# Two passes over the input channels in a layer's first projection, with its modulation rows read by column halves

## The chip, the cores and the metric

The program runs on one core of one Trainium2 chip. The metric is the device time of one execution in microseconds, the median of several runs. Besides its span (first to last instruction) an execution has a little more time around it. The engines are named as in the profile: PE is TensorE, with PEld for its weight loads, DVE is VectorE, ACT is ScalarE, POOL is GpSimd, SP is SyncE, which here only issues DMAs.

## What is computed

Two transformer layers over 256 tokens of width 2048, batch 1, in 32-bit floats. The change touches the start of the first:

```python
def hybrid_layer(x, c, rel_table, w_ada, b_ada, pre_g, post_g, w_in, sink,
                 w_pool_grp, pool_scale, w_br_attn, w_br_pool, w_merge, b_merge, w_out):
    mod = jax.nn.silu(c) @ w_ada + b_ada
    shift, scale, gate = jnp.split(mod, 3, axis=-1)
    h = rmsnorm(x, pre_g) * (1.0 + scale[:, None]) + shift[:, None]
    proj = h @ w_in
    q, k, v, gate_a, u, gate_p = jnp.split(proj, SPLIT_POINTS, axis=-1)
    ...
    g = jax.nn.sigmoid(h @ w_merge + b_merge)
    ...
    o = merged @ w_out
    return x + gate[:, None] * rmsnorm(o, post_g)
```

`w_ada` is 2048 x 6144 (its thirds give shift, scale and gate), `w_in` is 2048 x 4608. Nothing of `h @ w_in` can start before shift and scale are known for the input channels that it uses. The second layer has six such modulation vectors, from `w_mod`.

## The kernel before

**Weights.** Every large weight is read once, in slabs of 1 MB: 512 input channels (4 chunks of 128) by 512 columns. A slab lands in one of five slots of `w_stage` (SP, L557). ACT rounds it into `w_hi` (L779, two halves of 128x1024, three buffers), DVE takes the remainder, `w_lo = w_stage - w_hi` (`split_lo`, L1110, two halves). PE multiplies both, the three products of a split operand. SP issues slab n+3 while PE is at slab n, ACT and DVE split slab n+2 (`AHEAD`). `w_hi` of slab n+2 has to wait until PE has used slab n-1.

**Column groups.** `w_in` has nine groups of 512 columns, each four slabs deep, in the phases in 0, u0, u1, in 1 to 3, in_gates 0 and 1, gate_p1. A group fills all four banks of the tile `gemm` in PSUM, in two pairs. When a pair is complete ACT copies its low half into `proj` (L779), DVE adds the high half (L1501), and only then may PE start the next group in that pair (`wait_banks`). The first pair is complete in the middle of the group's last slab.

**Modulation.** A product with one row `c` is done on DVE: for each of the 16 chunks of channels one row of 128 x 2048 (1 MB) is read and accumulated with its `silu(c)` (`mod_acc`, L1088). 16 rows give a part, that is, one vector. PE then sums over partitions (16 products of 128x128 by 128x1, L1597 and L1842). Parts 0 and 1 (shift, scale) are done in the opening, 32 rows, through four of the slots of `w_stage`. Then come the 16 tiles of the operand: DVE scales (L1198), ACT makes the high part, DVE the low part (L1202). All later parts are hidden behind the matmuls: `mod_row` (L1104) reads a row in two halves of 512 KB through the two buffers of `mod_stage` (SP, L580), each reloaded once DVE has consumed it. `mod=(part, first row, rows)` and `slots` of a phase say at which slabs.

**What sets the order.** Each engine runs the same list of phases in order. At each slab DVE does `split_lo` of the slab two ahead, the phase's hooks (pooling, attention), its modulation row if any, and, at a group's last slab, the evacuation. SP issues the slab three ahead and then the modulation row. Phases after the nine: merge 0 to 7 (four slabs each, with one attention head hidden in each), branch1 0 to 3, out1 0 to 3, then the second layer.

## Time and profile before

| | us |
|---|---|
| median of 3 runs (2324.1 to 2327.34) | 2326.93 |
| the profiled execution | 2325.86 |
| its span | 2324.1 |
| PE busy / DVE busy / ACT busy in the span | 2217.0 / 1692.8 / 1062.4 |
| first matmul of `gemm` starts at | 106.94 |
| first matmul of the merge phases starts at | 330.71 |

PE is the busiest engine. A busy PE is not always a fast one: the rows of stretches carry the granted clock, 1.00 for its higher level (2.4 GHz) and 0.50 for its lower (1.2 GHz). Rows of a timeline say when a piece starts, how long it takes, and in brackets for how long the engine had been idle and what ended that.

### The profile page before, as it was taken

The numbers are of one execution on the slowest core, as the hardware profiler recorded it, in microseconds if no ns is written. First come the engines' busy times: TensorE is split into PE (matmuls) and PEld (weight loads), VectorE is DVE, ScalarE is ACT, GpSimd is POOL, SyncE is SP. The second block draws the span as 40 slices with busy tenths as digits, with TensorE's granted clock in tenths as the row PEclk, the third lists the DMA queues.
The fourth block names the chain that finished last, engine by engine and source line by source line (L and its number), as shares of the span: only waits on it lengthen the run. The fifth ranks groups of instructions, "written<-read, shape, count | busy, mean of one in ns | idle before, by whom it ended". The sixth has DMA issues, their size and how long they took to land.

```text
span 2324.1 us, 27765 instructions
## 1 busy us (share of the span) xinstructions
PE 2217.0 (95%) x11184; PEld 1863.6 (80%) x11184; DVE 1692.8 (73%) x1981; ACT 1062.4 (46%) x1345; POOL 74.7 (3%) x109
## 2 busy tenths in 40 slices
PE   5499999999999999999999999999999999999998
PEld 2388888888878878788878878878888888888886
DVE  6858867787777777767786887568888886774444
ACT  4143345554346654453455633455444443443432
POOL 0000000100000000000011100000000000000000
PEclk8599999999999999999999999999999999999999
DMA  9878778888985756669877888656676665657553
GB/s 381 332 249 299 277 259 312 297 313 309 313 289 198 252 173 227 233 204 329 288 268 242 286 319 277 237 201 216 218 242 229 235 219 175 204 182 253 188 193 127
DMA packets 244932, 583.49 MB, mean 251 GB/s; under 512 B 11994, under 2 KB 14830, under 8 KB 239428
## 3 DMA queue, kind: packets, MB, share of 16 engines
q1 hardware_dynamic: 232560, 535.93, 66.5%
q0 software_dynamic: 11104, 43.37, 5.5%
q10 hardware_dynamic: 1140, 2.43, 0.3%
q8 instruction: 88, 1.44, 0.2%
q14 instruction: 40, 0.33, 0.0%
HBM read 562.78 MB, written 18.90 MB: 250 GB/s over the span
## 4 chain that ended last, share of the span: by engine, by line
PE 79%; DVE 10%; DMA 7%; ACT 2%; issue 1%; ACTq 0%; DVEq 0%
PE gemm L1816 22%; PE gemm L1777 13%; PE gemm L1779 13%; PE gemm L1778 13%; PE gemm L1817 11%; DVE w_lo L1110 3%; DMA mod_stage<-in_w_mod 3%; DMA w_stage<-in_w_ada 2%; DVE mod_acc L1104 2%; DMA mod_stage<-in_w_ada 1%; PE gemm L1820 1%; PE extra L1597 1%; DVE mod_acc_scale L1088 1%; PE gemm L1819 1%; ACT w_hi L779 1%
## 5 line engine op out<-in xcount | busy, mean ns | idle before, releaser
L1110 DVE TENSOR_TENSOR w_lo<-w_stage,w_hi 128x1024 fp32r<-128x1024 f32 x730 | 861.5, 1223 | 432.5 <-ACT w_hi L779 432.1
L779 ACT ACTIVATE w_hi<-w_stage 128x1024 fp32r<-128x1024 f32 x730 | 731.4, 1051 | 831.1 <-PE gemm L1779 403.8
L1816 PE MATMUL gemm<-operand_main,w_hi 128*128 128x512 f32 x2535 | 912.3, 402 | 15.8 <-DVE proj L1501 14.4
L1817 PE MATMUL gemm<-operand_main,w_lo 128*128 128x256 f32 x2535 | 715.1, 282 | 0.0
L1816 PEld LDWEIGHTS gemm<-operand_main,w_hi 128*128 128x128 f32 x2535 | 480.7, 190 | 129.9 <-DVE w_lo L1110 15.3
L1817 PEld LDWEIGHTS gemm<-operand_main,w_lo 128*128 128x128 f32 x2535 | 483.1, 191 | 7.5
L1777 PE MATMUL gemm<-w_hi,operand_main 128*128 128x512 f32 x960 | 381.6, 398 | 7.3 <-DVE operand_main L1262 5.8
L1778 PE MATMUL gemm<-w_lo,operand_main 128*128 128x512 f32 x960 | 376.4, 392 | 0.0
L1779 PE MATMUL gemm<-w_hi,operand_main 128*128 128x512 f32 x960 | 376.1, 392 | 0.0
L1104 DVE SCALAR_TENSOR_TENSOR mod_acc<-mod_stage,c_silu,mod_acc 128x1024 f32<-128x1024 f32 x180 | 229.0, 1299 | 58.6 <-DMA mod_stage<-in_w_mod 43.0
L1777 PEld LDWEIGHTS gemm<-w_hi,operand_main 128*128 128x128 f32 x960 | 181.8, 189 | 46.9 <-issue 9.8
L1779 PEld LDWEIGHTS gemm<-w_hi,operand_main 128*128 128x128 f32 x960 | 181.8, 189 | 38.2
L1778 PEld LDWEIGHTS gemm<-w_lo,operand_main 128*128 128x128 f32 x960 | 181.9, 189 | 37.0
L1777 PE MATMUL gemm<-w_hi,ffn_hidden 128*128 128x512 f32 x352 | 136.9, 389 | 0.0
L1778 PE MATMUL gemm<-w_lo,ffn_hidden 128*128 128x512 f32 x352 | 136.9, 389 | 0.0
L1779 PE MATMUL gemm<-w_hi,ffn_hidden 128*128 128x512 f32 x352 | 136.9, 389 | 0.0
L1777 PE MATMUL gemm<-w_hi,operand_attn 128*128 128x512 f32 x256 | 101.6, 397 | 2.1 <-DVE w_lo L1110 2.1
L1778 PE MATMUL gemm<-w_lo,operand_attn 128*128 128x512 f32 x256 | 101.0, 395 | 0.0
L1779 PE MATMUL gemm<-w_hi,operand_attn 128*128 128x512 f32 x256 | 100.9, 394 | 0.0
L1779 PEld LDWEIGHTS gemm<-w_hi,ffn_hidden 128*128 128x128 f32 x352 | 66.1, 188 | 13.8
L1778 PEld LDWEIGHTS gemm<-w_lo,ffn_hidden 128*128 128x128 f32 x352 | 66.1, 188 | 13.8
L1777 PEld LDWEIGHTS gemm<-w_hi,ffn_hidden 128*128 128x128 f32 x352 | 66.1, 188 | 13.5
(231 smaller groups left out, 1744.5 us busy)
## 6 DMA issues: line engine op xcount, KB each, us to landing
w_stage<-in_w_in SPq DMA_DIRECT2D x129, 1024.0 KB, 6.2
mod_stage<-in_w_mod SPq DMA_DIRECT2D x192, 512.0 KB, 6.1
w_stage<-in_w_up SPq DMA_DIRECT2D x88, 1024.0 KB, 5.0
w_stage<-in_w_down SPq DMA_DIRECT2D x44, 1024.0 KB, 5.0
w_stage<-in_w_merge SPq DMA_DIRECT2D x32, 1024.0 KB, 6.1
w_stage<-in_w_out SPq DMA_DIRECT2D x32, 1024.0 KB, 7.8
w_stage<-in_w_ada SPq DMA_DIRECT2D x31, 1024.0 KB, 7.6
mod_stage<-in_w_ada SPq DMA_DIRECT2D x32, 512.0 KB, 6.0
```

The costliest lines, as they stand in the source:

```text
L779: return nc.scalar.activation(o, i_, f, **kw)
L1088: ins = stt(acc[:, c0:c1], row, CSI[:, t % 16:t % 16 + 1], acc[:, c0:c1], ALU.mult, ALU.add)
L1104: stt(acc, MST[:, half, :], CSI[:, c:c + 1], acc, ALU.mult, ALU.add).then_inc(mod_rows, 1)
L1110: tt(WL[:, slot_of(n), c0:c1], WST[:, slot_of(n), c0:c1], WH[:, n % HIS, c0:c1].bitcast(F32), ALU.subtract)\
L1597: ins = mm(X[3][:, t:t + 1], acc[:, t * P:(t + 1) * P], ONES[:, 0:1], start=True, stop=True)
L1777: mm(o, x_hi, hi, start=(k == 0), stop=False)
L1778: mm(o, x_hi, lo, start=False, stop=False)
L1779: ins = mm(o, x_lo, hi, start=False, stop=(k == nk - 1))
L1816: mm(G[:, m, :], hi, x_of(k), start=(k == 0), stop=False)
L1817: ins = mm(G[:, m, T:2 * T], lo, x_of(k)[:, 0:T], start=False, stop=False)
L1819: mm(G[:, m, T:2 * T], lo, x_of(k)[:, 0:T], start=False, stop=False)
L1820: ins = mm(G[:, m, :], hi, x_of(k), start=False, stop=True)
```

## The change

The rows of `w_ada` that are needed first are read by column halves. In the opening 16 rows are read instead of 32: each has the first 1024 columns of shift and the first 1024 of scale. That gives shift and scale for input channels 0 to 1023, operand tiles 0 to 7. The nine groups of `w_in` then run twice. Pass one (phases "half" 0 to 8) takes slabs 0 and 1 of each group and leaves the partial sum in `proj` (`part`). Under its first sixteen slabs the second halves of the 16 rows are read, two pieces of 512 KB each, through four buffers (`ada_stage`), and accumulated by DVE (`second_half`). In phase half 8 PE sums them over partitions (`ada_end`), and tiles 8 to 15 follow (`tiles`). Pass two takes slabs 2 and 3 of each group; its evacuation is done by DVE alone, two additions per pair (`rest`). The gate rows (part 2), which stood at 16 slabs of these nine groups, have 5 places left in pass two; the other 11 move into merge 0 to 3, and the rows of parts 3 and 4 move back behind them: merge 0 to 7 take 24 rows (16 before), branch1 0 to 3 take 12 (8 before), out1 7 (8 before). The column sums of part 2 move from the end of gate_p1 to the end of merge 3, those of part 3 from merge 7 to branch1 0. In the opening the eight products for the position bias (`line_rows`) are made in three portions with two buffers, and four products of the identity with `line_rows` are put before the column sums, into a bank that nobody reads. On POOL's queue the loads for the pooling now wait for operand tile 15, and the store of the bias lines stands behind them.

```diff
+        half = lambda c: Group(w_in, c, 2, "main", "part", tile=c // P)
+        rest = lambda c: Group(w_in, c, 2, "main", "rest", chunk0=KT // 2, tile=c // P)
...
-        pool = lambda n: {0: [("pool_sum", n)], 1: [("pool_mix", n)], 2: [("pool_out", n)]}
-        phases.append(Phase("in", 0, [one(0)]))
-        phases.append(Phase("u0", 0, [one(2560)]))
-        phases.append(Phase("u1", 0, [one(3072)]))
+        first_cols = (0, 2560, 3072, 512, 1024, 1536, 2048, 3584, 4096)
+        for n, c in enumerate(first_cols):
+            phases.append(Phase("half", n, [half(c)], ada=2 * n if n < 8 else None,
+                                hooks={0: [("ada_end", 0)], 1: [("ada_end", 1), ("tiles", 2)]} if n == 8 else {}))
+        phases.append(Phase("in", 0, [rest(0)], mod=(2, 0, 1), slots=(0,), hooks={0: [("tiles", 3)]}))
+        phases.append(Phase("u0", 0, [rest(2560)], mod=(2, 1, 1), slots=(0,)))
+        phases.append(Phase("u1", 0, [rest(3072)], mod=(2, 2, 1), slots=(0,)))
         for n, c in enumerate((512, 1024, 1536)):
-            phases.append(Phase("in", n + 1, [one(c)], mod=(2, 3 * n, 3), slots=(0, 2, 1), hooks=pool(n)))
-        for i in range(2):
-            phases.append(Phase("in_gates", i, [one(2048 + 1536 * i)], mod=((2, 9, 3), (2, 12, 3))[i],
-                                hooks={} if i else pool(3), post=[]))
-        phases.append(Phase("gate_p1", 0, [one(4096)], mod=(2, 15, 1), slots=(1,), post=[("mod_end", 2), ("silu1", 0), ("v1", 0)]))
+            phases.append(Phase("in", n + 1, [rest(c)], hooks={0: ([("pool_out", n - 1)] if n else []) + [("pool_sum", n)], 1: [("pool_mix", n)]}))
+        phases.append(Phase("in_gates", 0, [rest(2048)], hooks={0: [("pool_out", 2), ("pool_sum", 3)], 1: [("pool_mix", 3)]}))
+        phases.append(Phase("in_gates", 1, [rest(3584)], hooks={0: [("pool_out", 3)]}, mod=(2, 3, 1), slots=(0,)))
+        phases.append(Phase("gate_p1", 0, [rest(4096)], mod=(2, 4, 1), slots=(0,), post=[("silu1", 0), ("v1", 0)]))
...
-                                mod=(3, 2 * i, 2), slots=(0, 2),
-                                post=[("mod_end", 3)] if i == 7 else []))
+                                mod=(2, 5 + 3 * i, 3) if i < 3 else ((2, 14, 2), (3, 0, 3), (3, 3, 3), (3, 6, 3), (3, 9, 4))[i - 3],
+                                slots=(0, 1, 2, 3) if i != 4 else (1, 2, 3), post=[("mod_end", 2)] if i == 3 else []))
...
-                                hooks=behind, mod=(4, 2 * i, 2), slots=(0, 2)))
+                                hooks=behind, mod=(4, 3 * i - 3, 3) if i else (3, 13, 3), slots=(0, 1, 2),
+                                post=[] if i else [("mod_end", 3)]))
...
-                                hooks=behind, mod=(4, 8 + 3 * i, (3, 3, 2, 0)[i]), post=[("resid", 0)] if i == 3 else []))
+                                hooks=behind, mod=(4, (9, 12, 14, 16)[i], (3, 2, 2, 0)[i]), post=[("resid", 0)] if i == 3 else []))
...
-        MOD0_ROWS = 32
+        MOD0_ROWS = 16
...
+        AST = [MST[:, 0, :], MST[:, 1, :], proj_tile("ada_stage2", [P, D // 2], F32, 36)[:, :], proj_tile("ada_stage3", [P, D // 2], F32, 44)[:, :]]
...
+                src = w.rearrange("(c q) (p n) -> c q p n", q=P, n=D)[t, :, 0:2, 0:D // 2]
+                dst = WST[:, t % ROW_SLOTS, :].rearrange("q (p n) -> q p n", p=2)
...
+            def load_second_half(r):
+
+                if r == 0:
+                    sp.wait_ge(x_sq, 2)
+                for part in range(2):
+                    j = 2 * r + part
+                    positive(sp, ada_rows, j - 3)
+                    sp.dma_start(AST[j % 4], A["w_ada"][0].rearrange("(c q) n -> c q n", q=P)[r, :, part * D + D // 2:(part + 1) * D])\
+                        .then_inc(ada_landed[j % 4], 16)
...
+                if part == 2 and row0 + r == 0:
+                    sp.wait_ge(ada_rows, 32)
...
             for n in range(1, LEAD):
                 load_slab(n)
+                load_second_half(n - 1)
             for ph in phases:
                 for s in range(len(ph.slabs)):
                     if ph.slab0 + s + LEAD < len(slabs):
                         load_slab(ph.slab0 + s + LEAD)
+                    if ph.ada is not None and ph.ada + s + 2 < KT:
+                        load_second_half(ph.ada + s + 2)
                     for r in mods_behind(ph, s):
                         load_mod_row(ph, r)
...
-            pool.wait_ge(slab_used, 2)
-            pool.wait_ge(line_copied, HEADS1)
-            pool.dma_start(lines[:, 0:P * LINE].rearrange("h (q k) -> q h k", q=P), LINEB[:, :, :]).then_inc(start["lines_stored"], 16)
             pool.wait_ge(vec_copied, NP)
-            pool.wait_ge(start["lines_stored"], 16)
+            pool.wait_ge(ada_rows, 32)
+            pool.wait_ge(op_ready, op_count["prep_h0b"])
             pool.dma_start(WP[:, :, :, :], A["w_pool_group"][0].rearrange("g (c q) d -> q g c d", q=P))\
                 .then_inc(start["pool_in"], 16)
             pool.dma_start(INVC[:, :, :].rearrange("q g n -> q (g n)"), A["k_invcnt"][0].partition_broadcast(P))\
                 .then_inc(start["pool_in"], 16)
+            pool.wait_ge(line_copied, HEADS1)
+            pool.dma_start(lines[:, 0:P * LINE].rearrange("h (q k) -> q h k", q=P), LINEB[:, :, :]).then_inc(start["lines_stored"], 16)
 
...
+                    make_lines(7, HEADS1)
+                    act.wait_ge(half_modv, 2)
+                    high_tiles(0)
+                    split_hi(1)
+                    high_tiles(1)
+                    split_hi(2)
                     split_hi(3)
...
+            def second_half(r):
+
+                for part in range(2):
+                    j = 2 * r + part
+                    dve.wait_ge(ada_landed[j % 4], 16 * (j // 4 + 1))
+                    positive(dve, ada_rows, j - 1)
+                    acc = MACC1[:, part * (D // 2):(part + 1) * (D // 2)]
+                    if r == 0:
+                        ins = ts(acc, AST[j % 4], CSI[:, 0:1], None, ALU.mult)
+                    else:
+                        ins = stt(acc, AST[j % 4], CSI[:, r:r + 1], acc, ALU.mult, ALU.add)
+                    ins.then_inc(ada_rows, 1)
...
-            first_rows(0, 25)
+            first_rows(0, 13)
             norm_rs(0)
-            stage_mod_end(0)
-            first_rows(25, 28)
+            first_rows(13, 15)
             split_lo(0)
-            first_rows(28, MOD0_ROWS)
+            first_rows(15, MOD0_ROWS)
...
                 if what == "prep_h" and k == 0:
-                    base = 0
-                    src, src0, shift = PROJ, XT0, 0
                     scale_half(0)
...
+                    scale_tile(0)
+                    half_sums(0, 0)
+                    scale_tile(1)
+                    for t in range(2, 10):
+                        if t < 8:
+                            scale_tile(t)
+                        low_tile(t - 2)
+                        if t == 7:
+                            split_lo(1)
+                    split_lo(2)
+                    split_lo(3)
...
+                if name == "ada_end" and arg == 1:
+                    scale_half(1)
+                    half_sums(1, 0)
+                if name == "tiles":
+                    if arg == 2:
+                        scale_tile(8)
+                        scale_tile(9)
+                    for t in range(4 * arg, 4 * arg + 4):
+                        if t + 2 < KT:
+                            scale_tile(t + 2)
+                        low_tile(t)
...
-                    dve.wait_ge(lo_out, g.low0 + u + 1)
-                    if g.evac == "proj":
+                    if g.evac != "rest":
+                        dve.wait_ge(lo_out, g.low0 + u + 1)
+                    if g.evac in ("proj", "part"):
                         o = PROJ[:, g.kw["tile"] + 2 * u:g.kw["tile"] + 2 * u + nt, :]
+                        tt(o, high, o, ALU.add).then_inc(pair_done, 1)
+                    if g.evac == "rest":
+                        o = PROJ[:, g.kw["tile"] + 2 * u:g.kw["tile"] + 2 * u + 2, :]
+                        wait_evac(dve, part_of[g.col], u + 1)
+                        wait_full(dve, g, u)
+                        link(tt(o, half_of(g, u, 1), o, ALU.add))
                         tt(o, high, o, ALU.add).then_inc(pair_done, 1)
...
+                    if ph.ada is not None:
+                        second_half(ph.ada + s)
...
+                if name == "ada_end" and arg == 0:
+                    pe.wait_ge(ada_rows, 32)
+                    pe.wait_ge(half_modv, 2)
+                    ada_sums(MACC1, 1, 1, mod_summed)
+                    ada_sums(MACC1, 1, 0, mod_summed)
...
-            mod_end(0)
-            for half in range(2):
-                pe.wait_ge((half_row, mod0_rows)[half], (1, MOD0_ROWS)[half])
-                if half:
-                    pe.wait_ge(line_copied, HEADS1)
-                for t in range(8 * half, 8 * half + 8):
-                    ins = mm(X[2 - half][:, t:t + 1], MACC1[:, t * P:(t + 1) * P], ONES[:, 0:1], start=True, stop=True)
-                ins.then_inc((half_summed, mod_summed)[half], 1)
+            pe.wait_ge(mod0_rows, LAST_ROW - 1)
+            pe.wait_ge(line_copied, HEADS1)
+            for n in range(4):
+                mm(X[0][:, :], IDENT[:, :], LINEB[:, n, :], start=True, stop=True)
+            pe.wait_ge(half_row, 1)
+            ada_sums(MACC, 0, 1, half_summed)
+            pe.wait_ge(mod0_rows, MOD0_ROWS)
+            ada_sums(MACC, 0, 0, half_summed)
```

The opening on DVE, before: 32 rows (the first two entries of each part's 16, then `w_lo` of slab 0 between rows), then the sums' results `mod_cols` and the operand tiles.

```order
L1086 TENSOR_SCALAR mod_acc<-w_stage,c_silu 128x2048
L1088 SCALAR_TENSOR_TENSOR mod_acc<-w_stage,c_silu,mod_acc 128x2048 x15
L1086 TENSOR_SCALAR mod_acc_scale<-w_stage,c_silu 128x2048
L1088 SCALAR_TENSOR_TENSOR mod_acc_scale<-w_stage,c_silu,mod_acc_scale 128x2048 x8
L1115 RECIPROCAL rstd<-rstd 128x256
L1070 TENSOR_TENSOR mod_cols<-extra,columns 128x16
L1088 SCALAR_TENSOR_TENSOR mod_acc_scale<-w_stage,c_silu,mod_acc_scale 128x2048 x3
L1110 TENSOR_TENSOR w_lo<-w_stage,w_hi 128x1024 x2
L1088 SCALAR_TENSOR_TENSOR mod_acc_scale<-w_stage,c_silu,mod_acc_scale 128x2048 x3
L1088 SCALAR_TENSOR_TENSOR mod_acc_scale<-w_stage,c_silu,mod_acc_scale 128x1024 x2
L1136 TENSOR_TENSOR mod_cols<-extra,columns 128x8
```

And after:

```order
L1124 TENSOR_SCALAR mod_acc<-w_stage,c_silu 128x2048
L1126 SCALAR_TENSOR_TENSOR mod_acc<-w_stage,c_silu,mod_acc 128x2048 x12
L1166 RECIPROCAL rstd<-rstd 128x256
L1126 SCALAR_TENSOR_TENSOR mod_acc<-w_stage,c_silu,mod_acc 128x2048 x2
L1161 TENSOR_TENSOR w_lo<-w_stage,w_hi 128x1024 x2
L1126 SCALAR_TENSOR_TENSOR mod_acc<-w_stage,c_silu,mod_acc 128x1024 x2
L1185 TENSOR_TENSOR mod_cols<-extra,columns 128x8
L1194 SCALAR_TENSOR_TENSOR affine_cols<-mod_cols,columns 128x8
L1202 SCALAR_TENSOR_TENSOR quad_work<-proj,affine_cols,rstd 128x256
L1185 TENSOR_TENSOR mod_cols<-extra,columns 128x8
L1202 SCALAR_TENSOR_TENSOR quad_work<-proj,affine_cols,rstd 128x256 x2
L1207 SCALAR_TENSOR_TENSOR operand_main<-quad_work,mod_cols,operand_main 128x256
```

Half of the row instructions are gone from ahead of `mod_cols`; the reciprocal, `w_lo` and the tiles stand as close to the end of the rows as before.

The steady part of the nine groups on DVE, before (two groups without modulation rows: u0 and u1):

```order
L1110 TENSOR_TENSOR w_lo<-w_stage,w_hi 128x1024 x4
L1501 TENSOR_TENSOR proj<-gemm,proj 128x512 x2
L1110 TENSOR_TENSOR w_lo<-w_stage,w_hi 128x1024 x8
L1501 TENSOR_TENSOR proj<-gemm,proj 128x512 x2
L1110 TENSOR_TENSOR w_lo<-w_stage,w_hi 128x1024 x8
L1501 TENSOR_TENSOR proj<-gemm,proj 128x512 x2
```

After, in pass one (one group of two slabs and the start of the next):

```order
L1161 TENSOR_TENSOR w_lo<-w_stage,w_hi 128x1024 x2
L1139 SCALAR_TENSOR_TENSOR mod_acc_second_half<-mod_stage,c_silu,mod_acc_second_half 128x1024 x2
L1161 TENSOR_TENSOR w_lo<-w_stage,w_hi 128x1024 x2
L1139 SCALAR_TENSOR_TENSOR mod_acc_second_half<-ada_stage_97,c_silu,mod_acc_second_half 128x1024
L1139 SCALAR_TENSOR_TENSOR mod_acc_second_half<-ada_stage_98,c_silu,mod_acc_second_half 128x1024
L1575 TENSOR_TENSOR proj<-gemm,proj 128x512 x2
L1161 TENSOR_TENSOR w_lo<-w_stage,w_hi 128x1024 x2
```

Between the last `w_lo` of a group and the additions that free its banks (`proj<-gemm,proj`) now stand two row pieces, and a group ends after two slabs, not four.

The start of the merge phases' second head on DVE, before:

```order
L1104 SCALAR_TENSOR_TENSOR mod_acc<-mod_stage,c_silu,mod_acc 128x1024 x2
L1110 TENSOR_TENSOR w_lo<-w_stage,w_hi 128x1024 x2
L1387 TENSOR_TENSOR y_work<-extra,proj 128x256
L1392 TENSOR_TENSOR operand_attn<-y_work,operand_attn 128x256
L1358 SCALAR_TENSOR_TENSOR scores<-extra,bias 128x512
L1362 TENSOR_REDUCE small<-scores 128x2
L1367 TENSOR_SCALAR small<-small,sinks 128x2
L1110 TENSOR_TENSOR w_lo<-w_stage,w_hi 128x1024 x2
L1373 TENSOR_TENSOR small<-small 128x2
L1375 RECIPROCAL small<-small 128x2
L1380 TENSOR_SCALAR scores<-scores,small 128x256 x2
L1104 SCALAR_TENSOR_TENSOR mod_acc<-mod_stage,c_silu,mod_acc 128x1024 x2
```

After:

```order
L1155 SCALAR_TENSOR_TENSOR mod_acc<-mod_stage,c_silu,mod_acc 128x1024 x2
L1161 TENSOR_TENSOR w_lo<-w_stage,w_hi 128x1024 x2
L1460 TENSOR_TENSOR y_work<-extra,proj 128x256
L1465 TENSOR_TENSOR operand_attn<-y_work,operand_attn 128x256
L1431 SCALAR_TENSOR_TENSOR scores<-extra,bias 128x512
L1435 TENSOR_REDUCE small<-scores 128x2
L1440 TENSOR_SCALAR small<-small,sinks 128x2
L1155 SCALAR_TENSOR_TENSOR mod_acc<-mod_stage,c_silu,mod_acc 128x1024 x2
L1161 TENSOR_TENSOR w_lo<-w_stage,w_hi 128x1024 x2
L1446 TENSOR_TENSOR small<-small 128x2
L1448 RECIPROCAL small<-small 128x2
L1453 TENSOR_SCALAR scores<-scores,small 128x256 x2
```

Each merge phase has one more row of two pieces, behind the attention step at its second slab.

## Rows read from the trace of the kernel before

**Rows 1.** page: busy by engine; the group of line 779: busy us, mean ns
```profile
PE 2217.0 (95%) x11184; PEld 1863.6 (80%) x11184; DVE 1692.8 (73%) x1981; ACT 1062.4 (46%) x1345; POOL 74.7 (3%) x109
...
L779 ACT ACTIVATE w_hi<-w_stage 128x1024 fp32r<-128x1024 f32 x730 | 731.4, 1051 | 831.1 <-PE gemm L1779 403.8
```

**Rows 2.** TensorE in order of time, opening: start us, us, line, operation
```profile
100.10 6.99 PE L1842 MATMUL extra<-ones,mod_acc_scale 128*128 128x1 f32 x32 [32.50 <-DVE mod_acc_scale L1088]
...
106.94 0.77 PE L1816 MATMUL gemm<-operand_main,w_hi 128*128 128x512 f32 x1
```

**Rows 3.** VectorE in order of time, opening
```profile
45.41 12.27 DVE L1088 SCALAR_TENSOR_TENSOR mod_acc<-w_stage,c_silu,mod_acc 128x2048 f32<-128x2048 f32 x5 [0.15 <-DMA w_stage<-in_w_ada]
...
80.08 1.75 DVE L1115 RECIPROCAL rstd<-rstd 128x256 f32<-128x256 f32 x1
...
89.13 2.35 DVE L1110 TENSOR_TENSOR w_lo<-w_stage,w_hi 128x1024 fp32r<-128x1024 f32 x2
...
103.71 0.17 DVE L1136 TENSOR_TENSOR mod_cols<-extra,columns 128x8 f32<-128x8 f32 x1 [2.47 <-PE extra L1842]
...
105.30 0.48 DVE L1202 SCALAR_TENSOR_TENSOR operand_main<-quad_work,mod_cols,operand_main 128x256 fp32r<-128x256 f32 x1
```

**Rows 4.** VectorE in order of time, ends of two quiet column groups
```profile
150.44 2.36 DVE L1110 TENSOR_TENSOR w_lo<-w_stage,w_hi 128x1024 fp32r<-128x1024 f32 x2 [3.30 <-ACT w_hi L779]
...
152.75 0.69 DVE L1501 TENSOR_TENSOR proj<-gemm,proj 128x512 f32<-128x512 f32 x1
...
175.36 0.69 DVE L1501 TENSOR_TENSOR proj<-gemm,proj 128x512 f32<-128x512 f32 x1
```

**Rows 5.** VectorE in order of time, end of a group with modulation rows
```profile
250.19 1.28 DVE L1104 SCALAR_TENSOR_TENSOR mod_acc<-mod_stage,c_silu,mod_acc 128x1024 f32<-128x1024 f32 x1 [2.34 <-DMA mod_stage<-in_w_ada]
...
251.39 2.35 DVE L1110 TENSOR_TENSOR w_lo<-w_stage,w_hi 128x1024 fp32r<-128x1024 f32 x2
...
253.66 1.28 DVE L1501 TENSOR_TENSOR proj<-gemm,proj 128x512 f32<-128x512 f32 x2
```

**Rows 6.** TensorE in order of time: two waits for banks, and sums of columns
```profile
202.66 0.47 PE L1816 MATMUL gemm<-operand_main,w_hi 128*128 128x512 f32 x1 [0.96 <-DVE proj L1501]
...
254.49 0.47 PE L1816 MATMUL gemm<-operand_main,w_hi 128*128 128x512 f32 x1 [2.90 <-DVE proj L1501]
...
326.83 3.63 PE L1597 MATMUL extra<-ones,mod_acc 128*128 128x1 f32 x32
```

**Rows 7.** stretches: us, busy of PE, PEld, DVE, ACT, POOL, clock, DMA share, GB/s
```profile
110.00:115.00 5.00, 5.00 (x23) 4.30 (x22) 5.00 (x10) 2.99 (x7) 0.00 (x0) 0.74 0.00 0
...
202.00:203.00 1.00, 0.34 (x2) 0.33 (x3) 1.00 (x2) 1.00 (x2) 0.00 (x0) 1.00 1.06 424
...
256.00:257.00 1.00, 1.00 (x4) 0.86 (x4) 1.00 (x2) 0.00 (x0) 0.00 (x0) 0.50 1.04 391
...
331.00:335.00 4.00, 4.00 (x12) 3.15 (x11) 4.00 (x2) 4.00 (x4) 0.00 (x0) 0.57 0.16 61
```

**Rows 8.** DMA issues: out<-in, queue, count, KB each, median us to landing
```profile
w_stage<-in_w_in SPq DMA_DIRECT2D x129, 1024.0 KB, 6.2
...
mod_stage<-in_w_mod SPq DMA_DIRECT2D x192, 512.0 KB, 6.1
...
w_stage<-in_w_ada SPq DMA_DIRECT2D x31, 1024.0 KB, 7.6
```

**Rows 9.** who waited for whom, 200 to 310: us in total, times, longest
```profile
PE gemm L1816 <- DVE proj L1501: 5.3, 5, 2.9
```

**Rows 10.** stretches of a merge phase, and of the second and last branch phase
```profile
379.00:403.00 24.00, 24.00 (x110) 19.92 (x108) 18.62 (x23) 13.73 (x18) 2.13 (x4) 1.00 0.89 308
...
571.00:583.00 12.00, 12.00 (x54) 9.95 (x53) 10.82 (x12) 4.02 (x4) 0.53 (x1) 1.00 0.95 351
...
619.00:631.00 12.00, 12.00 (x58) 9.98 (x57) 11.93 (x13) 4.99 (x6) 1.24 (x2) 1.00 1.05 398
```

**Rows 11.** TensorE in order of time, out1 phase
```profile
645.19 0.76 PE L1777 MATMUL gemm<-w_hi,operand_main 128*128 128x512 f32 x1 [3.87 <-DVE operand_main L1262]
```

154 lines of the change are left out of this document (81 added, 73 removed).

## The prediction, made before the changed kernel was run

> **What bounds the kernel now.** I read the page first: PE is busy for 95% of the span [rows 1], so time is to be had where PE is empty or slow. The largest such place is the opening. PE's first matmul of the projection starts at 106.94; ahead of it PE summed columns for 6.99 us and before that sat idle for 32.50 us, waiting for DVE's `mod_acc_scale` [rows 2]. DVE at that time works without a break on 1 MB rows, five of them in 12.27 us, 2.45 us each [rows 3]. So the start is set by 32 rows, and each row less is worth 2.45 us. Next I read the ends of column groups: quiet ones repeat every 22.61 us (152.75 to 175.36) [rows 4], which is 5.65 us per slab; where modulation rows stand on DVE, PE waited for its banks, 5.3 us in five waits, the longest 2.9 us [rows 9]. Last I read the clock: the 0.96 us wait at 202.66 left the granted clock at 1.00, the 2.90 us wait at 254.49 was followed by 0.50 [rows 6, 7].
>
> **Opening.** The twelfth row starts at 45.41, so thirteen are done at 50.3 [rows 3]. The new order goes on with the reciprocal (1.75), two rows (4.9), `w_lo` (2.35): 59.3. The last row comes in two halves of 1.28 each [rows 5]; the scale half is done at 60.6, the shift half at 61.9. Eight column sums take half of 6.99 us at the low clock [rows 2] or half of 3.63 us at the high one [rows 6]. I take the high one: four 128x512 products now run just before, and in the kernel before the projection's own matmuls brought the clock from 0.50 back up within the stretch from 110 to 115 [rows 7]. The sums end at 60.6 + 1.8 + 1.8 = 64.2. From `mod_cols` to the end of the first low tile it was 105.30 + 0.48 - 103.71 = 2.1 us [rows 3], with two scalings now moved behind; I take 1.7. The first matmul starts at 65.9, **41.0 us earlier**; at the low clock it would be 69.4, 37.5 earlier. The bias lines leave this path: they are done before the rows, as now.
>
> **Start of pass one.** Now DVE has to bring seven more tiles (an estimate of 0.8 us each for two instructions of 0.48 that overlap [rows 3]), `w_lo` of slabs 1 to 3 (3 x 2.3), and four row pieces (two plain ones at 0.7, two at 1.25, estimates from rows 5) before it frees the first bank: 65.9 + 5.6 + 6.9 + 3.9 = 82.3. PE restarts 0.83 us after the addition begins (253.66 to 254.49 [rows 5, 6]): 83.1. Its own work of two slabs would end at 65.9 + 11.3 = 77.2. That is 5.9 lost, plus a clock drop, as after the 2.90 us wait. I price a drop by the stretch from 331 to 335 at 0.57, 43% of 4 us, 1.7 [rows 7]. Against it, before, the projection itself began at 0.50: clock 0.74 over 110 to 115 [rows 7] puts the rise at 112.6, so 2.8 us of loss are gone. Together **+4.8**.
>
> **The seven further group ends of pass one.** A slab's end lets ACT round the next high part (1.05 us a half [rows 1]), so `w_lo` starts about 1.2 us after it and takes 2.31 us to the next instruction [rows 4]: 3.5. Before, the addition followed at once. Now two row pieces, 2.5 us, stand between: the addition begins 6.0 and PE restarts 6.8 us after the slab's end, where the slab needs 5.65. Each group loses 1.15 us, **+8.1** in all. Such a gap is like that of 202.66, so no clock drop. The low bound is 0 (waits vanish); the high bound comes from loads. Each slab's issue on SP now stands behind a row piece that waits for a buffer. DVE consumes the group's last piece 5.65 + 6.0 = 11.7 us after the group's start; then the slab for the next critical place is issued, and it is needed when the next group has used its first slab, at 12.45 + 5.65 = 18.1, 6.4 us later. Landing takes a median 6.2, in the opening's full queue 7.6 [rows 8]; at 7.6 it is 1.2 us more per group, 16.5 in all.
>
> **Column sums in phase half 8.** 16 products, 3.63 us [rows 6], now inside the stream, and with a clock drop like the one that followed them at 331 [rows 7], 1.7 us: **+5.3**. Nothing hides them, PE is the engine that they occupy. DVE uses the time: tiles 8 to 11 end before the slab does.
>
> **Pass two.** DVE needs two additions of 0.69 [rows 4] per pair, begins 3.5 us after a slab's end and is done at 5.0, within 5.65. So 0.6 us cover is left, and the 5.3 us of bank waits [rows 9] with one clock drop (1.7) go, as no rows stand at the end of those groups. I leave 0.6 for the pooling groups: **-6.4**. ACT loses its copies there. POOL's loads for the pooling are issued once tile 15 is made, some 25 us before they are read; the 2 MB store of the lines follows them and shares the DMA with slabs that have about 5 us in hand. At the end of gate_p1 the sums of part 2 are gone (their cost comes back at merge 3, net 0), and they had covered the last evacuation: the transposes of v now wait for it, **+1.7** (two additions and the hand-overs).
>
> **The moved rows.** 24 rows stand in the merge phases (16 before), 12 in branch1 (8). A merge phase has DVE busy for 18.62 of 24 us [rows 10], so a third row of 2.5 fits. But a row can be loaded only after the one before is consumed, 6.1 us to landing [rows 8] and 1.3 for the first piece: one row per 7.4 us at best, against 6 us per slab. Three in four slabs fit (22 of 24). The four of merge 7 and three of branch1 0 stand at seven slabs in a row: 52 us against 46, so the last comes some 3 us late for PE's sums of part 3, which now stand right behind it. In branch1 1 to 3 DVE was busy 10.82 of 12 us and the DMA share was 0.95 [rows 10]: with 2.5 us more per 21.8 there is no air, and I put 2 us on each, 6 together. Two clock drops, 2. Behind waits of DVE stand the operand splits that out1 waited for already (3.87 us at 645.19 [rows 11], DVE 11.93 of 12 busy ahead of it [rows 10]). Sum **+11**; bounds 0 (the idle fifth of DVE takes it all) and 18 (3.5 per branch phase, 6 at the sums). I stay near the middle, since the merge row shows air and the branch rows none.
>
> **Sum.** -41.0 + 4.8 + 8.1 + 5.3 - 6.4 + 1.7 + 11.0 = -16.5. The profiled execution took 2325.86 (span 2324.1), 1.1 under the median of 2326.93. So 2309.4 on its scale, **2310** on the median's.
>
> **What the skill says.** The row shows that a bank wait of about 1 us left the clock at 1.00 [rows 6, 7]. The Trainium skill ("TensorE: Matmul & The Clock Gate", section "A second HAM failure mode: psum-queue depth-cycling") tells of a kernel in which frequent micro-idles between groups made the clock swing between its levels. By that rule the clock would fall at each of the seven group ends; by the row it does not, and the sum goes by the row. For a 512 KB row the skill ("DMA: Bandwidth & Descriptors", section on the anatomy of one DMA) gives about 2 us plus the bytes at 436 GB/s, an estimate of 3.2 us; rows would then never be late and the sum would be near 2300. The trace has 6.1 us.
>
> **Rivals.**
> The moved rows cost next to nothing: for it speak 5.4 us of idle DVE per merge phase, against it the branch rows. The last term is 1 instead of 11: 2300. Chance 0.20.
> The clock falls at each group end of pass one, as each recurs after 12.5 us and not alone as at 202.66: 7 x 1.7 = 12 more, 2322. Chance 0.08.
> The moved rows upset the attention steps too, which DVE does behind them: 10 more, 2320. Against it: a head's results are not wanted for a slab. Chance 0.10.
> Slower than before: in pass one the slabs arrive late, since SP issues them behind row pieces that wait for DVE, and DVE waits for the slabs. At 7.6 us to landing [rows 8] it is 1.2 more per group; waits pass 2 us and the clock falls each time: 8 + 12 = 20, which eats the gain of 16.5, 2330; at 9 us it is 2340. It decides from about 7.4 us on. Against it: 4 MB per 12.5 us are 336 GB/s where 391 to 424 were moved [rows 7]. Chance 0.07.
> That the opening doesn't shorten can't be: half of the rows are gone from ahead of the sums.
>
> **From these to the numbers.** The forecast (2303 to 2316) has 0.53, with 0.02 for nothing I named. 2296 to 2322 takes in the opening's low clock (+3.5) and both ends of the moved rows but for the outer tails. A measurement can tell about 0.2%, 4.7 us, from no change: faster than 2322.3 are the forecast, the first and third rival and half of the second, 0.87; within 0.2% 0.06; slower 0.07.
>
> **What would show it.** Right: the first `gemm` matmul near 66, line 1126 on DVE 14 times and then two halves; seven PE waits on `proj` of about 1 us, 12.5 apart, the clock 1.00 through them; one long wait near 78 to 83; the merge phases beginning near 300 instead of 330.7; PE waits in branch1 0 to 3 that were not there. Wrong: DVE's row pieces of line 1139 waiting for DMA, ACT's `w_hi` waiting for DMA in pass one, or branch phases that still last 21.8 us.

## The result and the profile after

The changed kernel takes 2350.34 us, the median of four runs (2344.84 to 2354.36), beside 2325.51 of the kernel before (2322.86 to 2327.34). The ratio is 1.0098, with a 95% interval of 1.0076 to 1.0119: **25 us slower**, where 16 us faster was forecast. The profiled execution is the slowest of the four, 2354.36 us with a span of 2352.6.

Five landmarks on TensorE cut both traces into the same stages: the first matmul of the projection; the first product of head 0's scores (start of merge 0); the same of head 7 (in merge 7); the last transposes of the merged rows (in out1 0); the last transposes of the normed rows (start of kv2). The names of the stages are rough: the stage "merge" ends at head 7's scores, so the stage "branch1" also holds the rest of merge 7.

| stage (us) | before | changed | difference | forecast |
|---|---|---|---|---|
| opening, to the first matmul | 106.94 | 67.13 | -39.8 | -41.0 |
| the projection's nine groups | 230.94 | 264.90 | +34.0 | +8.2 |
| merge 0 to 7 | 167.88 | 174.75 | +6.9 | +5.3 and part of 11 |
| branch1 0 to 3 | 125.29 | 145.87 | +20.6 | the rest of 11 |
| out1 | 112.57 | 110.52 | -2.1 | 0 |
| all that follows | 1580.48 | 1589.43 | +9.0 | 0 |

The 8.2 are the forecast's terms for both passes, 13.5, less the sums of part 2 and their clock drop (5.3), which reappear in the merge phases. The last row is no effect of the change that I can show: in the eighteen profiled executions of this study it lies between 1580.5 and 1589.4, whatever the kernel, and the changed kernel's other three runs are 4 to 10 us shorter. Another warning on scatter: experiment 5 leaves the projection as it is in the changed kernel, and its trace has 259.79 us there. So the question is where 26 us went in the projection and some 11 in branch1.

TensorE in order of time at the opening and at the first group ends of pass one (start us, us, line, operation, and the idle time before it):

```profile
67.13 0.77 PE L1918 MATMUL gemm<-operand_main,w_hi 128*128 128x512 f32 x1 [1.53 <-DVE operand_main L1207]
...
83.59 0.47 PE L1918 MATMUL gemm<-operand_main,w_hi 128*128 128x512 f32 x1 [2.46 <-DVE proj L1575]
...
100.81 0.76 PE L1918 MATMUL gemm<-operand_main,w_hi 128*128 128x512 f32 x1 [5.70 <-DVE proj L1575]
...
116.03 0.47 PE L1918 MATMUL gemm<-operand_main,w_hi 128*128 128x512 f32 x1 [1.08 <-DVE proj L1575]
...
132.23 0.77 PE L1918 MATMUL gemm<-operand_main,w_hi 128*128 128x512 f32 x1 [4.78 <-DVE proj L1575]
...
161.91 0.77 PE L1918 MATMUL gemm<-operand_main,w_hi 128*128 128x512 f32 x1 [3.36 <-DVE proj L1575]
```

The first two are the forecast's to within 1.2 us: the first matmul at 67.13 (forecast 65.9, before 106.94 [rows 2]), the restart after the first group at 83.59 (forecast 83.1). Then the groups should have followed every 12.45 us. They follow after 17.2, 15.2, 16.2, 14.9, 14.8, 14.6 and 14.6 us. One whole period, on DVE, ACT and SP:

```profile
161.08 1.28 DVE L1575 TENSOR_TENSOR proj<-gemm,proj 128x512 f32<-128x512 f32 x2
163.39 2.36 DVE L1161 TENSOR_TENSOR w_lo<-w_stage,w_hi 128x1024 fp32r<-128x1024 f32 x2 [1.03 <-ACT w_hi L801]
165.67 2.48 DVE L1139 SCALAR_TENSOR_TENSOR mod_acc_second_half<-mod_stage,c_silu,mod_acc_second_half 128x1024 f32<-128x1024 f32 x2
171.02 2.36 DVE L1161 TENSOR_TENSOR w_lo<-w_stage,w_hi 128x1024 fp32r<-128x1024 f32 x2 [2.88 <-ACT w_hi L801]
173.30 2.48 DVE L1139 SCALAR_TENSOR_TENSOR mod_acc_second_half<-ada_stage,c_silu,mod_acc_second_half 128x1024 f32<-128x1024 f32 x2
175.69 1.28 DVE L1575 TENSOR_TENSOR proj<-gemm,proj 128x512 f32<-128x512 f32 x2
```

```profile
162.30 2.00 ACT L801 ACTIVATE w_hi<-w_stage 128x1024 fp32r<-128x1024 f32 x2 [3.12 <-DMA w_stage<-in_w_in]
169.93 2.02 ACT L801 ACTIVATE w_hi<-w_stage 128x1024 fp32r<-128x1024 f32 x2 [5.62 <-DMA w_stage<-in_w_in]
```

```profile
160.00 1.52 SPq L587 DMA_DIRECT2D ada_stage<-in_w_ada  x2
161.56 0.43 SPq L563 DMA_DIRECT2D w_stage<-in_w_in  x1
166.97 1.53 SPq L587 DMA_DIRECT2D mod_stage<-in_w_ada  x2
168.54 0.43 SPq L563 DMA_DIRECT2D w_stage<-in_w_in  x1
174.61 1.52 SPq L587 DMA_DIRECT2D ada_stage<-in_w_ada  x2
```

Read as a circle: SP issues the slab at 161.56. It has landed when ACT rounds it at 169.93, 8.37 later. DVE makes its low part from 171.02 (1.09) to 173.38 (2.36), and the first row piece by 174.61 (1.23). That piece frees a buffer and SP issues its load; the second load waits in turn for DVE's second piece and goes out at 175.80; only behind both, at 176.18 (1.57), comes the next slab of this kind, two slabs later. 8.37 + 1.09 + 2.36 + 1.23 + 1.57 = 14.62, the period. TensorE is no part of the circle. Who waited for whom from 80 to 200 (us in total, times, longest) says the same; in the kernel before, ACT's `w_hi` waited 98.4 us for TensorE in the projection and 0.7 us for a slab:

```profile
ACT w_hi L801 <- DMA w_stage<-in_w_in: 50.0, 12, 6.5
DVE w_lo L1161 <- ACT w_hi L801: 38.5, 15, 5.8
...
PE gemm L1918 <- DVE proj L1575: 23.3, 8, 5.7
```

The waits decide the clock too. Stretches behind those of 5.70, 1.08, 4.78 and 1.07 us (columns as in [rows 7]; the number ahead of the DMA share is the granted clock):

```profile
100.00:106.00 6.00, 5.19 (x16) 4.45 (x17) 3.82 (x6) 2.00 (x2) 0.00 (x0) 0.50 0.99 353
116.00:121.00 5.00, 4.96 (x29) 4.42 (x30) 3.08 (x4) 2.01 (x2) 0.00 (x0) 1.00 0.91 322
132.00:138.00 6.00, 5.77 (x19) 4.99 (x20) 5.18 (x6) 2.01 (x2) 0.00 (x0) 0.54 0.84 298
147.00:152.00 5.00, 4.87 (x28) 4.31 (x29) 4.28 (x5) 2.01 (x2) 0.00 (x0) 1.00 0.87 304
```

### The profile page after: what moved, and what is told of

Same layout as the page of the kernel before. It is cut to its first block, busy times and chain, and to the rows that moved or that the text cites. A ratio compares the mean times of both kernels' runs of the same rounds, so it can differ in the third digit from the quotient of the medians.

```text
span 2352.6 us, 27894 instructions
## 1 busy us (share of the span) xinstructions
PE 2242.3 (95%) x11192; PEld 1882.1 (80%) x11192; DVE 1713.3 (73%) x2034; ACT 1061.0 (45%) x1345; POOL 74.5 (3%) x109
## 4 chain that ended last, share of the span: by engine, by line
PE 74%; DVE 12%; DMA 9%; ACT 2%; issue 2%; ACTq 0%; SPq 0%; DVEq 0%
PE gemm L1918 21%; PE gemm L1879 12%; PE gemm L1881 12%; PE gemm L1880 12%; PE gemm L1919 10%; DMA mod_stage<-in_w_mod 5%; DVE w_lo L1161 4%; DVE mod_acc L1155 2%; DMA w_stage<-in_w_in 2%; PE gemm L1922 1%; PE extra L1687 1%; DMA w_stage<-in_w_ada 1%; ACT w_hi L801 1%; DVE mod_acc_second_half L1139 1%; PE gemm L1921 1%
## 5 line engine op out<-in xcount | busy, mean ns | idle before, releaser
L1918 PE MATMUL gemm<-operand_main,w_hi 128*128 128x512 f32 x2499 | 915.0, 406 | 41.1 <-DVE proj L1575 33.6
L1922 PE MATMUL gemm<-operand_main,w_hi 128*128 128x512 f32 x205 | 81.9, 399 | 0.0
L1881 PEld LDWEIGHTS gemm<-w_hi,ffn_hidden 128*128 128x128 f32 x352 | 66.1, 188 | 13.7
```

The source lines that it names most:

```text
L1881: ins = mm(o, x_lo, hi, start=False, stop=(k == nk - 1))
L1918: mm(G[:, m, :], hi, x_of(k), start=(k == 0), stop=False)
L1922: ins = mm(G[:, m, :], hi, x_of(k), start=False, stop=True)
```

## Experiments on pass one

Each comparison with the kernel before is made beside it on the same chip. Where I compare two other kernels, I take the difference of their ratios, or the stage between two landmarks, which is sharper since the 1580 us behind don't enter.

**1. The slab issued ahead of the pieces (e1_slab_ahead).** In pass one SP asks for a slab one step earlier, so ahead of the pieces that wait for DVE.

```diff
+            issued = LEAD
             for ph in phases:
                 for s in range(len(ph.slabs)):
-                    if ph.slab0 + s + LEAD < len(slabs):
-                        load_slab(ph.slab0 + s + LEAD)
+                    upto = ph.slab0 + s + LEAD + (1 if ph.ada is not None else 0)
+                    while issued <= min(upto, len(slabs) - 1):
+                        load_slab(issued)
+                        issued += 1
```

> The changed kernel with one thing moved: in pass one SP issues the load of a slab one step earlier, so ahead of the row pieces that wait for DVE to free their buffers. Theory A (the slab loads stand in SP's queue behind waiting row pieces, and DVE then waits for the slab, which closes a loop of 14.6 us per group): the groups of pass one fall from 14.6 to 16.2 us to 12.5 to 13, DVE's 5.3 us wait at the start of pass one is gone, the clock drops there go; about 20 us less than the changed kernel, 2330. Theory B (DVE's own work of a group, two low parts, four row pieces, two additions, with the hand-overs, sets 14.6 us): within 3 us of the changed kernel, 2350. Theory C (the DMA engines can't bring two slabs and two rows in 12.5 us): no gain either, but with ACT still waiting for DMA.

Measured: 2326.72 us, ratio 0.9998 (0.9985 to 1.0010), 23 less than the changed kernel. The groups follow every 12.5 to 12.6 us, and ACT waits for no slab from 75 to 190. Theory A holds, B and C fall: the same work on DVE and the same bytes fit 12.58 us. VectorE in one period:

```profile
121.74 1.28 DVE L1578 TENSOR_TENSOR proj<-gemm,proj 128x512 f32<-128x512 f32 x2
...
129.65 2.36 DVE L1164 TENSOR_TENSOR w_lo<-w_stage,w_hi 128x1024 fp32r<-128x1024 f32 x2 [1.76 <-ACT w_hi L804]
131.92 2.48 DVE L1142 SCALAR_TENSOR_TENSOR mod_acc_second_half<-ada_stage,c_silu,mod_acc_second_half 128x1024 f32<-128x1024 f32 x2
134.31 1.28 DVE L1578 TENSOR_TENSOR proj<-gemm,proj 128x512 f32<-128x512 f32 x2
```

The slabs landed hardly sooner for it: median 7.9 us from 95 to 190, 8.4 in the changed kernel. In the kernel before it is 5.7 in that stretch, where few rows stand, but 8.0 from 200 to 310, where modulation rows run. The line of experiment 1, then the two of the kernel before (mean rate and landing, 200 to 310):

```profile
w_stage<-in_w_in SPq DMA_DIRECT2D x15, 1024.0 KB, 7.9
...
DMA packets 13016, 32.00 MB, mean 291 GB/s; under 512 B 686, under 2 KB 686, under 8 KB 13008
w_stage<-in_w_in SPq DMA_DIRECT2D x16, 1024.0 KB, 8.0
```

**2. The pieces issued by POOL (e9_rows_by_pool).** The slabs keep their position in SP's order; the pieces leave it. Above it could have been the earlier request that helped.

```diff
+            pool.wait_ge(mod0_rows, MOD0_ROWS - 2)
+            for r in range(KT):
+                load_second_half(r)
...
-                    if ph.ada is not None and ph.ada + s + 2 < KT:
-                        load_second_half(ph.ada + s + 2)
```

> The changed kernel with the row pieces of pass one issued by POOL, which has nothing else to do then, and not by SP: the slabs' own positions in SP's order are as in the changed kernel, nothing is left out. Theory A (it is the place behind waiting row pieces in SP's queue that makes a slab late): as e1_slab_ahead, groups of 12.6 us, 23 less than the changed kernel, 2327. Rival (e1_slab_ahead gained because a slab was asked for a step earlier than LEAD says, not because it was freed of the wait): groups stay above 14 us, 2348.

Measured: 2326.88 us, 1.0000 (0.9985 to 1.0014), with additions at 109.18 and 121.66, 12.48 apart. The place in SP's queue is enough to explain the loss. The landing stayed at 8.3 us with the pieces on another queue, and in experiment 3, without the pieces, it was 5.1. So it is not the queue that makes a slab slow to land but the bytes under way with it:

```profile
w_stage<-in_w_in SPq DMA_DIRECT2D x15, 1024.0 KB, 8.3
ada_stage<-in_w_ada POOLq DMA_DIRECT2D x12, 512.0 KB, 6.6
```

**3. The floor, no pieces (e2_no_half_rows).** Rows 1 to 15 are left out of pass one.

```diff
-                        second_half(ph.ada + s)
+                        if ph.ada + s == 0:
+                            second_half(0)
```

> The changed kernel with the second halves of rows 1 to 15 left out, neither loaded nor accumulated in pass one (their modulation columns are wrong). It gives the floor of pass one in two passes. Theories A, B and C all expect groups of 11.3 to 11.6 us and 2350 - 30 = 2320. If the groups stay above 13 us, the passes themselves (additions into a finished half, banks) are at fault, not the rows, and the time stays near 2345.

Measured: 2314.69 us, 0.9940 (0.9923 to 0.9956), 37 less than the changed kernel; groups of 11.27 us (additions at 114.58 and 125.85). So two passes as such cost TensorE nothing in a group, and experiment 1 still pays 1.31 us a group for the pieces.

**4. Additions ahead of the pieces (e4_adds_first).** As experiment 1, and at a group's last slab DVE frees the banks first.

```diff
+                    if ph.ada is not None and q == g.slabs - 1:
+                        evac(g)
                     if ph.ada is not None:
                         second_half(ph.ada + s)
                     for r in mods_behind(ph, s):
                         mod_row(ph, r)
-                    if q == g.slabs - 1:
+                    if q == g.slabs - 1 and ph.ada is None:
                         evac(g)
```

> As e1_slab_ahead, and DVE makes the additions that free PE's banks ahead of the two row pieces of a group's last slab, not behind them. If in pass one the 2.4 us of the two pieces stand on PE's path at each of eight group ends, as the forecast has it (1.15 us lost per group), it is 8 to 12 us under e1_slab_ahead, 2320. If loads still decide, it is within 2 us of e1_slab_ahead.

Measured: 2313.36 us, 0.9940 (0.9917 to 0.9962), 13 less than experiment 1. The nine groups take 232.45 us from first matmul to merge 0, where they took 243.60 in experiment 1 and 230.97 without pieces: now the pieces cost 1.5 us in all, read from one execution of each. DVE works 108.21 of the 120 us from 80 to 200, the DMA share is 0.91, the clock 1.00. This version is faster than the kernel before, by 0.6%, and leaves nothing out.

```profile
80.00:200.00 120.00, 116.79 (x671) 100.94 (x670) 108.21 (x118) 53.30 (x65) 2.63 (x3) 1.00 0.91 330
```

## Experiments on the moved rows

Of these, the stage "branch1" (from head 7's scores to the last transposes of the merged rows) tells most. It scatters by some 3 us: it lies between 142.98 and 145.87 in the five traces with three rows and all their loads and work (the changed kernel and experiments 1 to 4), and between 123.78 and 126.98 in the six with two rows (5, 9, 12, 13, 14, 16).

| kernel | rows in a branch1 phase | merge stage | branch1 stage | whole, ratio |
|---|---|---|---|---|
| before | 2 | 167.88 | 125.29 | 1 |
| changed | 3 | 174.75 | 145.87 | 1.0098 |
| 5: changed, two rows | 2 | 173.02 | 126.93 | 0.9992 |
| 6: before, three rows in branch1 | 3 | 167.88 | 137.97 | 1.0050 |
| 4: additions first | 3 | 175.22 | 144.77 | 0.9940 |
| 7: of 4, third rows not loaded | 3 | 174.64 | 135.81 | 0.9908 |
| 8: of 4, third rows not added | 3 | 173.11 | 139.24 | 0.9931 |
| 9: of 4, two rows | 2 | 174.67 | 126.98 | 0.9855 |

**5. Two rows a phase (e3_two_rows).** In merge and branch1 phases each `mod` has two rows, at two of the four slabs; 12 rows are left out.

```diff
-                                mod=(4, 3 * i - 3, 3) if i else (3, 13, 3), slots=(0, 1, 2),
+                                mod=(4, 3 * i - 3, 2) if i else (3, 13, 2), slots=(0, 2),
```

> The changed kernel with two modulation rows in each merge and branch1 phase, as in the kernel before, where it has three or four; the 12 rows too many are left out of the computation. Theory A (the third row of a phase can only be loaded once the second is consumed, so DVE waits for it with the weights' low parts queued behind): the waits of PE in branch1 0 to 3 and at the sums there go, 15 to 20 us less than the changed kernel, 2333. As I priced these rows in the forecast: 11 less, 2339. Rival (the sums of part 3 and the splits of the operands cost this wherever they stand): under 5 less, 2346.

Measured: 2325.50 us, 0.9992 (0.9977 to 1.0007), 25 less. Of it 19 are in branch1 and 2 in the merge phases; 5 are in the projection, which the edit doesn't touch, and are scatter. My price of 11 was too low, and by far the most of it belongs to branch1.

**6. That part alone (e8_before_three_branch).** The kernel before, with three rows in each branch1 phase and four fewer in out1; nothing left out.

```diff
-                                hooks=behind, mod=(4, 2 * i, 2), slots=(0, 2)))
+                                hooks=behind, mod=(4, 3 * i, 3), slots=(0, 1, 2)))
...
-                                hooks=behind, mod=(4, 8 + 3 * i, (3, 3, 2, 0)[i]), post=[("resid", 0)] if i == 3 else []))
+                                hooks=behind, mod=(4, (12, 14, 15, 16)[i], (2, 1, 1, 0)[i]), post=[("resid", 0)] if i == 3 else []))
```

> The kernel before with one part of the change alone: three modulation rows in each of the four branch1 phases where it has two, and four fewer in out1; nothing is left out. My forecast priced a third row in such a phase at 2 us: 8 more, less 1 for out1, 2334. If DVE waits out the load of each third row (6 to 13 us in the changed kernel's trace), PE loses 3 to 4 us a phase: 12 to 16 more, 2340. If the loss of the changed kernel came from the sums of part 3 and the crowd at merge 7 and branch1 0 alone: within 3 us of the kernel before, 2327.

Measured: 2338.32 us, 1.0050 (1.0034 to 1.0067), 12 more. The branch1 stage is 12.7 longer and out1 3.8 shorter. The sums of part 3 stand where they stood, so this is the third row alone.

It is not an even price per phase. The stage in pieces, each from TensorE's first product on `operand_attn` to the first one of the next phase (out1's operand stands in that tile too; us):

| piece | before | changed | experiment 6 |
|---|---|---|---|
| rest of merge 7 | 22.95 | 19.26 | 22.94 |
| branch1 0 | 23.47 | 36.73 | 23.50 |
| branch1 1 | 21.76 | 24.15 | 21.76 |
| branch1 2 | 21.76 | 21.76 | 23.33 |
| branch1 3 | 23.54 | 30.39 | 31.81 |
| out1 0 up to its transposes | 11.81 | 13.58 | 14.63 |

TensorE waits little or not at all in the middle phases; the delay comes out where it needs something that stands behind the rows on DVE: the sums of part 3 in branch1 0, and out1's operands at the end of branch1 3.

**7, 8, 9. Load or work (e5_third_unloaded, e16_third_not_added, e15_two_rows).** What makes a third row dear, its load or DVE's 2.5 us? On the kernel of experiment 4, the third (and fourth) row of a phase is not loaded, while DVE still adds what stands in the buffer (7); is loaded and waited for, but only 8 columns of each half are added (8); is neither (9).

```diff
+                if not_loaded(ph, r):
+                    return
```

```diff
+                    n_cols = 8 if ph.name in ("merge", "branch1") and r >= 2 else D // 2
```

> As e4_adds_first, but the third and fourth rows of the merge and branch1 phases are not loaded; DVE accumulates what stands in the buffer once more (13 rows of the computation are wrong), so that its instructions stay the same in number and kind. Theory A (a row can be loaded only after the one before is consumed, and DVE waits for it with the low parts behind): nearly all that leaving the rows out gives comes back, 15 to 22 us less than e4_adds_first, 2295. Theory B (the third rows cost by the 2.5 us of DVE's work each): at most 5 less, 2310.

> As e4_adds_first, but of the third and fourth rows of the merge and branch1 phases DVE accumulates 8 columns of each half and not 1024 (13 rows are wrong); their loads and waits stay. e5_third_unloaded, the opposite, gave 8 us. If the loads' waits carry the cost (theory B): at most 5 less, 2309. If DVE's time carries it (theory C): 12 to 18 less, 2298. If the two add up, e15_two_rows lies lower by the sum of both; if they overlap, by less.

> As e4_adds_first (2313), with two rows in each merge and branch1 phase, the 12 further rows left out of load and computation (e3_two_rows on the mended base). If the extra rows cost the same as in the changed kernel: 25 less, 2288. If half of it was pass one's delay carried on: 12 less, 2301.

Measured: 2305.12 us, 0.9908 (0.9888 to 0.9927), without the loads; 2311.11 us, 0.9931 (0.9907 to 0.9956), without the work; 2297.18 us, 0.9855 (0.9828 to 0.9881), without both. The ratios of 7 and 8 are too near that of 4 for their intervals; the stage is clear. Over the 126.98 of two rows, the work alone adds 8.8 us, the load alone 12.3, both 17.8, a little less than their sum of 21.1. Neither theory was right alone: load and work each cost about 10 us by themselves. Which of them is the larger I can't say, as 3.5 us between two single traces is about what the stage scatters. Experiment 9 is 20 us under experiment 4 by the ratios, nearer to 25 than to 12, and in branch1 the rows cost 17.8 there and 18.9 on the changed kernel. The missing 5 us are those that experiment 5 had gained in the projection, which its edit didn't touch; so in the stages I see none of the cost as pass one's delay carried on.

VectorE in branch1 of the changed kernel shows both: the pieces wait 2.06 and 0.76 for their loads, and what stands behind them starts that much later.

```profile
588.58 2.36 DVE L1161 TENSOR_TENSOR w_lo<-w_stage,w_hi 128x1024 fp32r<-128x1024 f32 x2
593.00 1.28 DVE L1155 SCALAR_TENSOR_TENSOR mod_acc<-mod_stage,c_silu,mod_acc 128x1024 f32<-128x1024 f32 x1 [2.06 <-DMA mod_stage<-in_w_mod]
595.04 1.29 DVE L1155 SCALAR_TENSOR_TENSOR mod_acc<-mod_stage,c_silu,mod_acc 128x1024 f32<-128x1024 f32 x1 [0.76 <-DMA mod_stage<-in_w_mod]
596.24 2.35 DVE L1161 TENSOR_TENSOR w_lo<-w_stage,w_hi 128x1024 fp32r<-128x1024 f32 x2
```

TensorE feels it at three places that have no wait in the kernel before: in branch1 0, before the sums of part 3, and before out1's operands. The sums then run at the low clock, 6.98 us where the same sums took 3.63 before.

```profile
533.91 0.47 PE L1879 MATMUL gemm<-w_hi,operand_attn 128*128 128x512 f32 x1 [2.03 <-DVE operand_attn L1465]
...
555.92 6.98 PE L1687 MATMUL extra<-ones,mod_acc 128*128 128x1 f32 x32 [4.40 <-DVE mod_acc L1155]
...
639.07 0.77 PE L1879 MATMUL gemm<-w_hi,operand_attn 128*128 128x512 f32 x1 [6.70 <-DVE operand_attn L1335]
```

The three waits are 13.1 us. The low clock adds 3.4 in the sums, 2.4 in branch1 1 (granted clock 0.81 from 563 to 575) and 1.8 behind the last wait (0.87 from 639 to 652.65). Together these are the 20.6 us of the stage.

**10, 11. Is it SP's queue again (e12_moved_by_pool, e13_branch_by_pool)?** In branch1 ACT waits for slabs as it did in pass one. If these slabs are late because they stand behind waiting pieces, the cure of experiment 2 should work here. The modulation rows of merge and branch1 phases (10), or of branch1 alone (11), go by POOL; buffers and DVE's order stay as in experiment 4.

```diff
+                    if blk == 0:
+                        for r in range(ph.mod[2]):
+                            load_mod_row(ph, r)
                     load_gates(blk, 1, i)
```

> As e4_adds_first (2313), with the modulation rows of the merge and branch1 phases issued by POOL, not by SP; the same buffers, the same order on DVE, nothing left out. Theory A (slab loads queued behind waiting row pieces on SP): ACT's waits for slabs in these phases (99 us in e4_adds_first) go, and 10 to 18 us of time with them, 2299. Theory B (DVE waits for each row's own load, which starts only when the row before is consumed) or C (DVE's work): within 3 us, 2313. POOL's stores and loads of gates now stand behind rows, which could cost a few us.

> As e12_moved_by_pool, but only the rows of the four branch1 phases go by POOL. If the loss sits in branch1 (13.7 us of PE waits stood there and at its edges in the changed kernel), it is as good as e12_moved_by_pool or better; if merge phases lose too, it lies between it and 2313.

Measured: 2344.04 us, 1.0093 (1.0065 to 1.0120), and 2325.72 us, 0.9992 (0.9976 to 1.0008): 36 and 12 more than experiment 4, not less. Waits from 300 to 780 in experiment 4 and, below, in experiment 11:

```profile
DVE mod_acc L1158 <- DMA mod_stage<-in_w_mod: 38.2, 28, 8.3
...
ACT w_hi L804 <- DMA w_stage<-in_w_branch_pool: 15.3, 3, 7.9
```

```profile
DVE mod_acc L1179 <- DMA mod_stage<-in_w_mod: 42.0, 27, 5.5
...
ACT w_hi L825 <- DMA w_stage<-in_w_branch_pool: 7.8, 2, 4.1
```

ACT's waits for branch slabs fell (from 15.3 and 7.8 to 7.8 and 1.3 us, the second figures for the attention weights), DVE's waits for rows did not, the stage went from 144.77 to 148.00 and out1 from 111.18 to 118.34. So here the late slabs were a symptom: freeing them brought nothing. Why the sums of part 3 waited 8.2 us there and not 3.7 I did not take apart. In pass one the pieces have four buffers; here each half of a row has one, and its load begins when that half of the row before is consumed. That chain stays whichever engine issues it. The whole of the 36 us is not explained by it: the merge stage went to 191.86, where POOL's stores of gates and loads of bias lines now stood behind rows, a new wait that I put in and did not take apart.

## A placement that beats both

**12. Fewer rows where four slabs take 22 us (e6_spread).** As experiment 4, with the 48 rows placed anew: eight in pass two, 22 in the merge phases, two in each branch1 phase, ten in out1. Nothing is left out.

```diff
-                                mod=(2, 5 + 3 * i, 3) if i < 3 else ((2, 14, 2), (3, 0, 3), (3, 3, 3), (3, 6, 3), (3, 9, 4))[i - 3],
-                                slots=(0, 1, 2, 3) if i != 4 else (1, 2, 3), post=[("mod_end", 2)] if i == 3 else []))
+                                mod=((2, 8, 3), (2, 11, 3), (2, 14, 2), (3, 0, 3), (3, 3, 3), (3, 6, 3), (3, 9, 3), (3, 12, 2))[i],
+                                slots=(0, 1, 2) if i != 3 else (1, 2, 3), post=[("mod_end", 2)] if i == 2 else []))
...
-                                mod=(4, 3 * i - 3, 3) if i else (3, 13, 3), slots=(0, 1, 2),
+                                mod=(4, 2 * i - 2, 2) if i else (3, 14, 2), slots=(0, 2),
```

> As e4_adds_first, with the same 48 modulation rows placed otherwise: eight in pass two, 22 in the merge phases, two in each branch1 phase (as in the kernel before), ten in out1. Nothing is left out. If three rows in a phase of four slabs cost in branch1 (21.8 us, DVE at 11 of 12) and not in a merge phase (24 us), this is 12 to 18 us less than e4_adds_first, 2298. If rows cost the same wherever they stand, it is within 3 us of it, 2313.

Measured: 2299.66 us, 0.9890 (0.9863 to 0.9918). The branch1 stage is 125.35, as in the kernel before, and the merge stage, 173.08 with nearly three rows in each phase, is that of before plus the moved sums. In this trace a third row costs in branch1 and not in a merge phase. With the same merge placement the merge stage was longer in the traces of experiments 13, 16 and 14, 175.91, 178.50 and 180.41; in 16 and 14 TensorE waited several times there, up to 2.1 us, for attention's `probs_t`. Spread over six added rows, a third row in a merge phase costs between 0 and 1.2 us. This is **1.1% faster than the kernel before** and 2.1% faster than the changed one.

**13. Additions first in pass two as well (e7_spread_adds_first).**

```diff
-                    if ph.ada is not None and q == g.slabs - 1:
+                    early = g.evac in ("part", "rest")
+                    if early and q == g.slabs - 1:
```

> As e6_spread, and in pass two too the additions of a group stand ahead of the row at its last slab. Only one row stands at a last slab there, so 0 to 3 us less than e6_spread, 2297.

Measured: 2299.75 us, 0.9884 (0.9864 to 0.9903): the same. The projection stage shrank from 238.20 to 232.58, since a row no longer stands before the last evacuation of gate_p1, and the other stages gave it back.

**14. As 13, the store of the bias lines 50 us later and one row of gate_p1 moved (e11_store_later).**

```diff
             pool.wait_ge(line_copied, HEADS1)
+            pool.wait_ge(slab_used, [ph for ph in phases if ph.name == "in"][2].slab0)
             pool.dma_start(lines[:, 0:P * LINE].rearrange("h (q k) -> q h k", q=P), LINEB[:, :, :]).then_inc(start["lines_stored"], 16)
```

> As e7_spread_adds_first, with the 2 MB store of the bias lines issued by POOL some 50 us later in pass two (not together with the pooling weights), and one of the two rows of gate_p1 moved to the column group at 1536. Nothing is left out. The one PE wait of 3.0 us in pass two and its clock drop go, 3 to 4 us less, 2296. If the wait came from the pooling weights or from SP's own loads: within 2 us of 2300.

Measured: 2301.07 us, 0.9877 (0.9856 to 0.9897). The wait of 3.00 us, which stood at 216.19 in 13, is gone, and one of 1.18 stands at 254.58: the store beside the pooling weights was its cause, as the row that moved too stands later. The stage is 230.46, 2.1 less than in 13, and the merge stage 4.5 longer; as a whole no difference.

**15. Rows by POOL on that placement (e14_spread_by_pool)**, the change of 10 on kernel 14.

> As e11_store_later (2301), with the rows of the merge and branch1 phases issued by POOL. There the branch1 phases have two rows and PE waits little: by theory A 3 to 6 us less, 2296, from the splits at out1; by B and C the same, 2301.

Measured: 2320.58 us, 0.9977 (0.9962 to 0.9992), 23 more than 14. Between the two profiled executions, which lie 30 us apart, 19 are in the merge stage (199.77) and 8 in branch1 (133.43). It agrees with 10, not with theory A.

**16. Without the four products ahead of the sums (e10_no_products)**, on kernel 12.

```diff
-            pe.wait_ge(mod0_rows, LAST_ROW - 1)
             pe.wait_ge(line_copied, HEADS1)
-            for n in range(4):
-                mm(X[0][:, :], IDENT[:, :], LINEB[:, n, :], start=True, stop=True)
```

> As e6_spread without the four 128x512 products that PE does ahead of the first column sums; no result depends on them. As in the forecast: the sums run at the low clock (6.99 us in place of 3.73) and the first matmul of the projection comes 3.4 us later, 2303. If the products bring nothing, since the clock is low again at the first matmul anyway: within 1 us, 2300.

Measured: 2306.75 us, 0.9909 (0.9893 to 0.9926). The sums, with TensorE's idle time ahead of them, then the first matmul:

```profile
61.85 6.96 PE L1698 MATMUL extra<-ones,mod_acc 128*128 128x1 f32 x32 [8.96 <-DVE mod_acc L1129]
70.34 0.77 PE L1923 MATMUL gemm<-operand_main,w_hi 128*128 128x512 f32 x1 [1.54 <-DVE operand_main L1210]
```

The first matmul is 2.3 us later than in kernel 12 (68.00), whose sums took 4.54 us (3.73 in the changed kernel). The rest of the difference of 4 to 7 us lies in the merge stage (178.50 against 173.08), which the edit doesn't touch and where the traces scatter as much.

## Why the prediction was wrong

**Opening: right.** -41.0 was forecast, -39.8 measured. The sums took 3.73 us, as at the high clock. That the clock would then hold was wrong: behind the idle 1.53 us ahead of the first matmul it was 0.50 from 66 to 72. The forecast had counted the slow start of before, 2.8 us, as gone; it came again.

**Start of pass one: right in time, incomplete in cause.** The restart came at 83.59, forecast 83.1. DVE sets it, so by luck the slow start cost nothing: it only shortened TensorE's wait, 2.46 us where 5.9 was forecast. The clock drop of 1.7 that I had put behind the wait didn't come (1.00 from 84 to 90). But behind it DVE idled 5.32 us for slab 4, which SP issued only at 80.85, behind a piece that waited for row 0. The forecast had followed this engine's queue for the steady state and not for the start.

**Seven group ends: the term that failed.** The forecast had the right rival and the right budget, and then took the wrong row for the landing. Its budget, 6.4 us from the slab's issue to its need, is confirmed by the two traces: with groups of 12.58, as in experiment 1, the additions after those at 161.08 would come at 173.66; there ACT's rounding runs 5.75 us ahead of the additions (129.65 - 1.09 = 128.56 to 134.31), so at 167.9, 6.3 us after the issue at 161.56. The slab came after 8.37, 2.0 too late, and 12.58 + 2.0 is the 14.6 that was measured. I had set 6.2, the median over the whole kernel [rows 8], against 6.4 and called it in time; 7.6, from the only full queue in the rows, stood beside it and belonged in the sum, as pass one puts 2 MB under way per slab step. The trace of before had a nearer value that I had not asked for: 8.0 from 200 to 310 at 291 GB/s, the very stretch of [rows 9], where rows and slabs share the queue. The rival "slabs arrive late", with waits over 2 us and a falling clock, is what happened, at a landing between the two that I priced (2330 at 7.6, 2340 at 9). I gave it 0.07. The argument against it, 336 GB/s needed where 391 to 424 were moved, spoke of bandwidth, and the loss was one of order: experiment 4 moved 330 GB/s in the same stretch, and TensorE's waits for banks there came to 3.2 us in all. The 1.15 us of the term itself was sound, 1.31 in experiment 1 against 3.

**Sums in half 8: right** (3.63 us, forecast 3.6, and the clock 0.72 from 200 to 206). The phase as a whole took 19.5 us and not 16.6, since it began behind a wait of 3.10 us with the clock at 0.66 from 191 to 196.

**Pass two and the transposes of v: right but for one place.** The transposes waited 1.58 (forecast 1.7). At 247.44 TensorE waited 3.39 us and the clock fell; a row and a slab were late while POOL's pooling weights and the 2 MB store of the lines were under way. I had named that load and given it nothing. Experiment 14 moved the store, and that wait went; the stage was 2.1 us shorter.

**Moved rows: a term too small, and in the wrong places.** I put 2 us on each of three branch phases, 3 on branch1 0, 2 for the clock and none on the merge phases: 11. Measured 20.6 for the stage of the branch phases and 1.6 for the merge phases (6.9 less the moved 5.3), so the rival that the attention steps are upset is not seen. The branch phases don't each lose 2: branch1 2 still lasts 21.76 us, branch1 1 loses only by the low clock, and the loss is 13.1 us of waits in branch1 0 and ahead of out1 and 7.5 of low clock, where I had 2. The branch price was worked out from DVE's busy share alone [rows 10]; it left out that the single buffer makes each row's load start only after the row before. I had written that very limit, a row per 7.4 us against 6 us per slab, and applied it only to where the rows run on into the sums. By experiments 7 and 8 load and work both count, each with about 10 us.

**In sum** the terms missed 22.1 us up to the end of pass one (forecast 83.1 + 1.7 for the clock drop + 7 x 12.45 + 11.3 + 5.3 = 188.6, measured 210.67), 4.9 in pass two (head 0's scores forecast for 305.0, measured 332.03) and 11 in the moved rows: -16.5 + 38 = +21.5. The measured median is +25; the remainder is within what the last stage scatters.

**On the clock.** In the changed kernel's projection waits of 1.08, 1.07, 1.78 and 2.46 us left the granted clock at 1.00, and those of 3.10, 3.36, 4.78 and 5.70 were followed by 0.50 to 0.77 over the next five or six us (0.50 was seen after 2.90 before, [rows 6, 7]). In experiment 1, with seven waits of 1.04 to 1.07 us, one every 12.5 to 12.6 us, the clock was 1.00 from 88 to 180. So the forecast's rival, that it would fall at each of seven short waits, is out. The opening is different, below. That rival was drawn from the Trainium skill, "TensorE: Matmul & The Clock Gate", section "A second HAM failure mode: psum-queue depth-cycling"; by it short idles between groups make the clock swing, and these traces disagree for idles of 1 to 2.5 us between column groups.

**On the landing.** The Trainium skill, "DMA: Bandwidth & Descriptors", section on the anatomy of one DMA, gives 2 us plus the bytes at 436 GB/s, an estimate of 4.4 us for a 1 MB slab. The fit there is for a single DMA that GpSimd issues; these are issued by SP, which neither the forecast nor this estimate allows for. The trace has 5.7 in the kernel before from 95 to 190 and 8.4 in pass one, where two further pieces are under way with each slab, and the measurement decides.

## What to carry to other kernels

Before adding loads to a queue that issues in order, write down for each older load what it now stands behind, and close the circle: wait, issue, landing, use, and the release that the wait is for. If that circle is longer than the stage's own period, it is the period, however idle the engines are. And take the landing from a stretch that is as full as the new one will be. A step with one buffer costs its load's latency as well as its work; put it where the phase is long (24 us took three rows at 0 to 1.2 us each), not where it is short (22 us took two). And don't look for its price in every phase: it came out where TensorE first needed something that stood behind the rows.

## What I had not expected of the hardware

A 1 MB slab takes as long to land whether 1 MB of row pieces was put on the same queue before it (8.4 us, and 7.9 when it is issued early) or on POOL's (8.3), and 5.1 without them. Filling the 16 DMA engines to a share of 0.91 did no harm by itself (experiment 4).

The length of an idle time is not all that goes with a fall of the clock. In the opening it was 0.50 behind the column sums (3.73 us) and 1.53 us of idle time, where 2.46 us behind a whole column group left 1.00. The idle time need not be the cause: in half 8 TensorE went from the same sums straight on to its matmuls, without a wait, and the clock still fell to 0.72. No run parts the sums from the idle time in the opening. The opening's stretch, then the sums of half 8 and the stretch around their end:

```profile
66.00:72.00 6.00, 4.87 (x15) 4.22 (x16) 5.51 (x14) 5.57 (x11) 0.00 (x0) 0.50 0.49 187
...
198.36 3.63 PE L1693 MATMUL extra<-ones,mod_acc_second_half 128*128 128x1 f32 x32
...
200.00:206.00 6.00, 6.00 (x33) 5.39 (x33) 5.93 (x14) 2.44 (x5) 0.00 (x0) 0.72 0.90 342
```
